# Down weights with four consecutive rows on one partition, gate and up columns taken with a step of four

## The reference, cut to what matters

```python
def swiglu(x, w_gate, w_up, w_down):
    return (jax.nn.silu(x @ w_gate) * (x @ w_up)) @ w_down
# per expert: w_gate, w_up [1024, 3584]; w_down [3584, 1024]; all float32
```

## Time and profile before

| | |
|---|---|
| time, median of 3 runs | 1525.81 us (1525.42 to 1528.82) |
| span of the profiled execution | 1527.9 us (the page gives no other time for it) |
| PE busy over the span | 1448.0 us (95%) |
| DVE, ACT, POOL busy | 653.7, 259.0, 30.3 us |
| DMA packets, data | 138184, 434.27 MB |
| mean granted TensorE clock | 0.973 |
| chain that ended last | PE 85%, DMA 6%, DVE 6%, ACT 3% |

### The profile page before, as it was taken

One profiled execution on the slowest core, in us unless ns is written; L12 is line 12 of the kernel. 1 busy time (PEld: TensorE's weight loads), 2 busy tenths in 40 slices (PEclk: granted clock), 3 DMA queues, 4 the chain that ended last, 5 costly groups with the idle time before them and its releaser, 6 DMA issues.

```text
span 1527.9 us, 46201 instructions
## 1 busy us (share of the span) xinstructions
PE 1448.0 (95%) x21517; PEld 1382.4 (90%) x21517; DVE 653.7 (43%) x1549; ACT 259.0 (17%) x441; POOL 30.3 (2%) x33
## 2 busy tenths in 40 slices
PE   7998999997986889999999999999999999999997
PEld 6857999997864778999999999999999999999996
DVE  6952554445467651343224224134224323332327
ACT  2333444434234210200000000000000000000001
POOL 0000000000000210000000000000000000000000
PEclk9998999999996999999999999999999999999998
DMA  9041655353330008699999999999999999999994
GB/s 312 30 166 56 220 206 181 128 198 124 126 109 1 3 3 321 236 392 406 408 395 406 409 388 408 408 381 408 408 380 410 408 376 409 406 386 408 408 373 169
DMA packets 138184, 434.27 MB, mean 284 GB/s; under 512 B 10108, under 2 KB 13286, under 8 KB 137863
## 3 DMA queue, kind: packets, MB, share of 16 engines
q1 hardware_dynamic: 133536, 420.59, 71.5%
q0 software_dynamic: 1472, 5.24, 1.0%
q10 hardware_dynamic: 2982, 5.45, 1.0%
HBM read 426.42 MB, written 4.85 MB: 282 GB/s over the span
## 4 chain that ended last, share of the span: by engine, by line
PE 85%; DMA 6%; DVE 6%; ACT 3%; issue 1%; SPq 0%; ACTq 0%; DVEq 0%
PE bank L2545 34%; PE bank L2543 18%; PE bank L2152 4%; PE bank L2154 4%; PE bank L2153 4%; DMA ring<-in_moe_w_up 4%; PE bank L1894 3%; PE bank L2222 3%; DMA ring<-in_moe_w_gate 2%; PE bank L2125 2%; PE bank L2140 1%; PE bank L2060 1%; PE bank L2145 1%; PE bank L2387 1%; DVE xnT L1083 1%
## 5 line engine op out<-in xcount | busy, mean ns | idle before, releaser
L2543 PE MATMUL bank<-ring,yT 128*32 128x384 f32 x5760 | 633.5, 490 | 7.0 <-DMA ring<-in_moe_w_gate 4.3
L2545 PE MATMUL bank<-ring,yT 128*32 128x128 f32 x5760 | 634.9, 273 | 0.0
L2545 PEld LDWEIGHTS bank<-ring,yT 128*32 128x32 f32 x5760 | 627.7, 110 | 0.4 <-issue 0.4
L2545 PE MATMUL bank<-ring,arena 128*32 128x128 f32 x2304 | 255.4, 273 | 0.0
L2543 PE MATMUL bank<-ring,arena 128*32 128x384 f32 x2304 | 255.2, 490 | 0.0
L2545 PEld LDWEIGHTS bank<-ring,arena 128*32 128x32 f32 x2304 | 251.4, 110 | 0.0
L1801 DVE TENSOR_TENSOR arena<-arena,bank 128x384 f32<-128x384 f32 x56 | 28.9, 551 | 430.6 <-PE bank L2545 286.7
L1749 DVE STREAM_TRANSPOSE arena<-arena 32x192 f32<-32x192 f32 x384 | 141.9, 370 | 114.3 <-PE bank L2545 109.3
L2543 PEld LDWEIGHTS bank<-ring,yT 128*32 128x32 f32 x5760 | 165.9, 108 | 9.7 <-issue 5.9
L2154 PE MATMUL bank<-arena_r,ring_r 128*128 128x256 f32 x608 | 171.5, 282 | 0.0
L2152 PE MATMUL bank<-arena_r,ring_r 128*128 128x256 f32 x528 | 148.0, 280 | 1.3 <-DVE arena_r L1329 1.3
(11 more groups left out here) (473 smaller groups left out, 1264.0 us busy)
## 6 DMA issues: line engine op xcount, KB each, us to landing
ring<-in_moe_w_gate SPq DMA_DIRECT2D x56, 2048.0 KB, 22.0
ring<-in_moe_w_up SPq DMA_DIRECT2D x56, 2048.0 KB, 22.1
ring<-in_moe_w_down SPq DMA_DIRECT2D x56, 2048.0 KB, 20.3
ring<-in_ffn_w_gate SPq DMA_DIRECT2D x5, 2048.0 KB, 7.9
ring<-in_ffn_w_up SPq DMA_DIRECT2D x5, 2048.0 KB, 8.1
ring<-in_ffn_w_down SPq DMA_DIRECT2D x5, 2048.0 KB, 8.6
ring<-in_o_w_in SPq DMA_DIRECT2D x5, 2048.0 KB, 7.7
ring<-in_e_w_in SPq DMA_DIRECT2D x4, 2048.0 KB, 16.9
```

The lines of the kernel that those rows point to most:

```text
L2543: pe_.matmul(b[QUAD[m], 0:FM], x(m), w[:, 0:FM], start=start, stop=stop, skip_group_check=True)
L2545: last = pe_.matmul(b[QUAD[3], P * m:P * m + P], x(m), w[:, FM:FB], start=start and m == 0, stop=stop, skip_group_check=True)
```

## The change

A down block's rows are laid out as (p k) instead of (k p): partition p gets rows 4p, 4p+1, 4p+2 and 4p+3 of the 512, which are 16 KB in one piece in HBM and land in one piece of 16 KB on the partition. Row group k of the block then holds rows 4n + k. To match, the columns of a gate or up step are seen as 128 groups of four, and `by_tokens` takes columns k, k+4, k+8 and so on as its k-th run of 128. It gets a view of three dimensions (`w[:, 0:3, :]`, `w[:, 3, :]`); for down blocks that view names the same consecutive columns as before. Nothing else changes: loads, waits, slots, the number and size of matmuls, the PSUM addresses, and the work of ACT and DVE stay.

```diff
-            src = src.rearrange("o (k p) n -> p (o k) n", p=P)
+            src = src.rearrange("o (p k) n -> p (o k) n" if kind == "down" else "o (k p) n -> p (o k) n", p=P)
...
             for m in range(3):
-                pe_.matmul(b[QUAD[m], 0:FM], x(m), w[:, 0:FM], start=start, stop=stop, skip_group_check=True)
+                pe_.matmul(b[QUAD[m], 0:FM].rearrange("p (j n) -> p j n", j=3), x(m), w[:, 0:3, :], start=start, stop=stop,
+                           skip_group_check=True)
             for m in range(3):
-                last = pe_.matmul(b[QUAD[3], P * m:P * m + P], x(m), w[:, FM:FB], start=start and m == 0, stop=stop,
+                last = pe_.matmul(b[QUAD[3], P * m:P * m + P], x(m), w[:, 3, :], start=start and m == 0, stop=stop,
                                   skip_group_check=True)
...
                         if kind == "down":
+                            cols = cols.rearrange("p (j n) -> p j n", j=4)
...
                         else:
                             kk = nk * x + k
+                            cols = cols.rearrange("p (n j) -> p j n", j=4)
```

## The result

The changed kernel takes 2165.24 us (median of four runs, 2162.80 to 2166.59) against 1527.24 us for the kernel before on the same chip (four runs, 1525.42 to 1528.82): 1.417 times as long, with a 95% interval of 1.4146 to 1.4199. It is 638 us slower, where 6.5 us less had been forecast.

What follows compares the result with a forecast made beforehand. The expert stage was taken as bound by TensorE's own streaming but for 6.5 us of waiting for loads. Removing those, with stepped reading at 0, gave 1525.8 - 6.5 = 1519.3 us; range 1514 to 2185, the likeliest case's own 1515 to 1524.

Steps and rivals of the forecast that it cites:

- Part 2, TensorE's reading: Gate and up steps: moving operand read 16 bytes from value to value, 688,000 column times in series; taken to add 0 us.
- The upper bound: Gate and up reading: if it paid like stepped DVE or ACT writes, 475 or 660 us more on 688,000 columns.
- every strided column costs a fetch of its own: Rival, gate and up steps: 1.3 us each instead of 0.65, 583 us more, 2102 us in all; chance 0.27.
- theory A: From the follow-ups: TensorE's moving operand opens a 16-byte line no oftener than once in about 1.77 ns.
- the forecast's 0.43: Chance given to the likeliest case, the whole kernel at 1519.3 us, faster by more than 3 us.
- The rule of the Trainium skill: On SBUF reads: lines of 16 bytes, at least two hits a line for full bandwidth; a step of four float32 has one.
- The four column groups disturb one another: Rival, gate and up steps: four streams use up one stream's reserve; a tenth on 585 us, 1578 us; chance 0.13.
- Part 1: Down loads in the expert stage: 16 KB runs at 423 GB/s, 0.19 us less a block, 10.7 us for all 56.
- the removed wait: TensorE's wait for gate and up loads, 1390 to 1480 us: all 6.5 us were to go.
- a small fetch queued between them waits longer: Token fetches between 16 KB packets (0.62 against 0.16 us): asked for many blocks ahead, so costed at 0.
- The size from the Trainium skill: Down loads: about three extra cycles a packet, an estimated 0.09 us a block and 5 us in all; not used.
- the signs for part 1: Down loads: DMA rate above 407 GB/s, landing times no longer growing to 25 us, TensorE busy for all of 1390 to 1480 us.

## Why the prediction was wrong

- **Part 2, TensorE's reading, was costed at 0. This step failed.** It was concluded from the earlier trace rows that a port which delivers contiguous fp32r values every 0.46 ns has reserve for stepped float32 values every 0.85 ns. The 0.46 ns are for values that share lines, four to a line, 1.84 ns for a line. Counted in lines, the same row shows one opened every 1.84 ns and none oftener: there was no evidence of reserve at all. The runs gave 1.77 ns a line, and even the stepped fp32r itself lost its pace (0.91 ns).
- **The upper bound was the right one.** Stepped writes of DVE and ACT had given 0.69 and 0.96 ns more a value. The extra here is (1.77 - 0.85) = 0.92 ns a column from the distance of starts, and 637 / 688,000 us = 0.93 ns from the stage. The argument against these rows, that they are writes of other engines, didn't hold: they come to 1.73 and 1.83 ns a value, and TensorE's read to 1.77.
- **The rival "every strided column costs a fetch of its own" came true**, in its mechanism (theory A) and in its place. Its price was taken as 0.85 ns more a column and was 0.93: 2165 us instead of 2102, within its own range of 1994 to 2180. It should have had more than the forecast's 0.43. The rule of the Trainium skill (SBUF — State Buffer, note on cachelines) that was cited for it is borne out for lines of 16 bytes and for float32 (two hits a line: 3 to 4% more; one hit: 2.1 times); what the same note calls a free reach, 4 fp32, is that second case and is not free. For bfloat16 two hits a line cost twice the time.
- **"The four column groups disturb one another" fell.** One stream and four have the same price, and each group has its own pace.
- **Part 1 had the right mechanism, sign and rate, and the removed wait was mis-sized.** The rate of 16 KB runs, extrapolated to 423 GB/s from 2 KB and 4 KB runs, was measured at 426. But "a small fetch queued between them waits longer" had been costed at 0, and the token fetches took 5.9 to 7.7 us instead of 2.8 to 4.0, with all loads slow meanwhile. Over the mixed stage the rate rose from 400 to 404 GB/s only. "I remove all of the 6.5 us" did not hold: 3.2 us of idle time remained. Why loads that landed 6.6 us earlier by the 151st (8.5 less the 1.9 of the stage's earlier start) did not end the wait altogether is not settled. The wide rows alone gained 6.9 us in the median (1529.68 to 1522.76) where 6.5 had been forecast, but the agreement is in part chance: the stage became 5.2 us shorter, and the rest lies outside it or within the spread of the runs. The size from the Trainium skill (DMA: Bandwidth & Descriptors, Why small descriptors are slow) was an estimate of 0.09 us a block. In the stretches of long runs alone a block takes 4.92 us instead of 5.15, 0.23 us less, and over the mixed stage 6.9 us by some 44 down blocks are 0.16, against the 0.19 of the prediction.
- **In the changed kernel part 1 is worth nothing**, since TensorE at 10.9 us for a gate or up block leaves the loads far behind as a limit (share 0.62). With the step alone it is 2162.5 us, without a gain from part 1 to be seen.
- **The signs named in advance** were 116,680 packets (116,679), longer `yT` groups beside unchanged `arena` groups (834 and 399 beside 492 and 273 ns), DMA engines falling idle, and sets no longer 0.33 us apart. Each came. Of the signs for part 1, read in the kernel with the wide rows alone, the rate above 407 GB/s came (426). Landing times below 25 us and a TensorE busy for all of 1390 to 1480 us (86.8 of 90) did not.

## What to carry to other kernels

Count the lines of 16 bytes that a moving operand opens, and give each 1.77 ns: float32 at the full clock needs two columns a line, bfloat16 four, and fp32r neither of the two steps tried. A rate seen with contiguous data is no evidence for stepped data. Where an order has to be permuted for wide loads, let an engine with slack do it (here DVE's transposes, at 93 us of busy time, of which some 1 us shows at the end), and look at each column group for itself, since one stepped group of four costs as much as all.

## What the runs showed of the hardware

- A line costs 1.77 ns for float32 and bfloat16 alike, at steps of 8, 12, 16 and 32 bytes. It is not lengthened when the granted clock falls to 0.50 (0.450 to 0.455 us for 256 lines at either level), and each column group has its own.
- fp32r costs 0.9 ns a column at a step of two and of four at the full clock, against 0.46 contiguous. At the granted clock of 0.50 a step of four adds nothing to the 0.43 us of 512 contiguous columns.
- 16 KB runs move 426 GB/s alone, where 4 KB runs move 407. A token fetch of 112 packets beside them takes 5.9 to 7.7 us instead of 2.8 to 4.0, at 312 to 335 GB/s for the core, and the whole stage gains 1%.
- DVE's transpose of 32 partitions takes 406 ns for 128 float32 columns read with a step of 16 bytes, longer than the 370 ns for 192 contiguous ones.
